# A third set of HGRN level operands, made one level earlier

## What is computed

```
def step(S, inp):
    qc, kc, vc, gc = inp
    b = jnp.cumsum(gc, axis=1)
    o_inter = jnp.einsum('bthk,bhkv->bthv', qc * jnp.exp(b), S)
    diff = b[:, :, None] - b[:, None, :]
    decay = jnp.where(tri, jnp.exp(jnp.where(tri, diff, 0.0)), 0.0)
    att = jnp.einsum('bthk,bshk,btshk->bhts', qc, kc, decay)
    o_intra = jnp.einsum('bhts,bshv->bthv', att, vc)
    b_last = b[:, -1]
    S = jnp.exp(b_last)[..., None] * S + jnp.einsum(
        'bshk,bshv->bhkv', kc * jnp.exp(b_last[:, None] - b), vc)
    return S, o_inter + o_intra
```

## Time and profile before

| | us |
|---|---|
| median of 3 runs | 1237.44 |
| lowest, highest | 1236.23, 1239.28 |
| profiled execution, its time | 1236.89 |
| its span, first to last instruction | 1235.1 |

### The profile page before, as it was taken

One profiled execution on the slowest core, in us unless ns is written; L12 is line 12 of the kernel. 1 busy time (PEld: TensorE's weight loads), 2 busy tenths in 40 slices (PEclk: granted clock), 3 DMA queues, 4 the chain that ended last, 5 costly groups with the idle time before them and its releaser, 6 DMA issues.

```text
span 1235.1 us, 22212 instructions
## 1 busy us (share of the span) xinstructions
PE 1146.0 (93%) x8917; PEld 1084.5 (88%) x8917; DVE 711.1 (58%) x1449; ACT 538.5 (44%) x950; POOL 182.3 (15%) x144
## 2 busy tenths in 40 slices
PE   5789999988999989999998999789999999999996
PEld 4688788966998978989988999589999999999996
DVE  5726554455487666476686655554463644636464
ACT  3433556456536555655535323453232232232334
POOL 1400000000133223213032001141011010110100
PEclk9889999999999988999998999799999999999997
DMA  9683322222322312222222155212323222222202
GB/s 313 199 315 103 103 69 93 80 73 77 136 84 71 105 42 64 71 67 73 71 69 71 62 192 185 69 35 69 103 69 103 69 76 96 70 102 70 92 12 77
DMA packets 108778, 120.46 MB, mean 98 GB/s; under 512 B 2692, under 2 KB 98652, under 8 KB 108389
## 3 DMA queue, kind: packets, MB, share of 16 engines
q1 hardware_dynamic: 108677, 119.06, 29.4%
HBM read 109.22 MB, written 11.80 MB: 98 GB/s over the span
## 4 chain that ended last, share of the span: by engine, by line
PE 47%; DVE 7%; ACT 2%; issue 1%; DMA 1%; POOL 0%; DVEq 0%; ACTq 0%; POOLq 0%
PE PS L763 41%; DVE wR L1288 1%; PE PS L877 1%; PE PS L722 1%; DMA xT<-residual 1%; DVE xhat L1256 1%; PE PS L923 1%; DVE qt L1441 0%; DVE tmp L1272 0%; PE PS L680 0%; DVE kt L1442 0%; DVE att L1459 0%; PE PS L930 0%; DVE tmp L1271 0%; PE PS L920 0%
## 5 line engine op out<-in xcount | busy, mean ns | idle before, releaser
L763 PE MATMUL PS<-hR,wR 128*128 128x288 f32 x3744 | 533.4, 300 | 12.8 <-ACT tmp L1069 6.7
L763 PEld LDWEIGHTS PS<-hR,wR 128*128 128x128 f32 x3744 | 509.5, 191 | 23.3 <-ACT tmp L1069 7.7
L763 PE MATMUL PS<-actR,wR 128*128 128x288 f32 x1920 | 258.8, 295 | 2.0 <-DVE actR L1425 1.8
L763 PEld LDWEIGHTS PS<-actR,wR 128*128 128x128 f32 x1920 | 255.4, 188 | 3.4 <-DVE actR L1425 2.0
L1288 DVE TENSOR_TENSOR wR<-raw,wR 128x512 fp32r<-128x512 f32 x256 | 205.0, 801 | 71.5 <-ACT wR L990 64.1
L990 ACT ACTIVATE wR<-raw 128x512 fp32r<-128x512 f32 x256 | 161.9, 632 | 140.6 <-PE PS L763 132.9
L1588 POOL TENSOR_TENSOR D<-b 128x512 f32<-128x512 f32 (+1 forms) x56 | 68.2, 1217 | 508.2 <-PE PS L850 267.9
L1615 POOL TENSOR_TENSOR actR<-tmp,actR 128x576 fp32r<-128x576 f32 x32 | 46.2, 1445 | 304.8 <-DVE actR L1341 304.8
L1341 DVE CAST actR<-tmp 128x576 fp32r<-128x576 f32 x32 | 15.2, 476 | 129.5 <-ACT tmp L1088 129.5
L722 PE MATMUL PS<-wR,hR 128*128 128x256 f32 x600 | 82.8, 296 | 2.0 <-ACT kT L1056 0.9
L722 PEld LDWEIGHTS PS<-wR,hR 128*128 128x128 f32 x600 | 77.5, 200 | 5.1 <-issue 1.7
(11 more groups left out here) (212 smaller groups left out, 1214.7 us busy)
## 6 DMA issues: line engine op xcount, KB each, us to landing
raw<-in_w_in SPq DMA_DIRECT2D x30, 1024.0 KB, 5.1
raw<-in_w_up SPq DMA_DIRECT2D x16, 1024.0 KB, 5.3
raw<-in_w_down SPq DMA_DIRECT2D x16, 1024.0 KB, 4.9
mid<-in_w_ada SPq DMA_DIRECT2D x12, 1024.0 KB, 5.1
ada<-in_w_ada SPq DMA_DIRECT2D x8, 1024.0 KB, 13.3
S<-in_state_hgrn SPq DMA_DIRECT2D x8, 512.0 KB, 4.5
out_hgrn_sample<-S SPq DMA_DIRECT2D x8, 512.0 KB, 5.2
raw<-in_w_out SPq DMA_DIRECT2D x4, 1024.0 KB, 4.9
```

The lines of the kernel that those rows point to most:

```text
L763: mm = pe.matmul(PS[:, 2 * x.pair + h, 0:HALF], weights(x, w, k, col), rhs[r], start=(k == 0 and n == 0), stop=(k == last and n == 2))
```

## The change

The operands get a third set (`qt2`, `kt2`), so the level uses set n % 3 in place of n % 2. In the slot of level n, `g_operands` is now for level n+2 (was n+1), `g_exp` for n+3 (was n+2) and `g_diff` for n+4 (was n+3). The second lead-in slot of a pair makes what is then missing: difference 3, operands 1 and exponential 2. The differences keep their three tiles, and the scores keep their two banks. `kt2` is cleared at its first use.

```
-    yield []
+    yield [("g_diff", first, 3), ("g_operands", first, 1), ("g_exp", first, 2)]
...
-                if n + 1 < 2 * NL:
-                    ev += [("g_operands", *at(n + 1))]
+                if n + 2 < 2 * NL:
+                    ev += [("g_operands", *at(n + 2))]
                 if k == 2:
                     ev += [("g_products", r)]
                 ev += [("g_level", r, k)]
-                if n + 2 < 2 * NL:
-                    ev += [("g_exp", *at(n + 2))]
                 if n + 3 < 2 * NL:
-                    ev += [("g_diff", *at(n + 3))]
+                    ev += [("g_exp", *at(n + 3))]
+                if n + 4 < 2 * NL:
+                    ev += [("g_diff", *at(n + 4))]
...
-                bank, q, k = A[l % 2], QTL[n % 2], KTL[n % 2]
+                bank, q, k = A[l % 2], QTL[n % 3], KTL[n % 3]
...
-                if n < 2:
+                if n < 3:
...
-                    done(dve.memset(KTL[n % 2][:], 0.0))
+                    done(dve.memset(KTL[n % 3][:], 0.0))
                 dve.wait_ge(s_E, n + 1)
-                if n >= 2:
-                    dve.wait_ge(s_lv, n - 1)
+                if n >= 3:
+                    dve.wait_ge(s_lv, n - 2)
```

More of the change, by code:

```diff
@@ L404, in program @@
             g_names += [(f"b{s}", [P, 2, TOK]), (f"kr{s}", [P, 2, TOK]), (f"qs{s}", [P, 2, TOK]), (f"rv{s}", [P, TT + 1, UC])]
-        (b0, kr0, qs0, rv0, b1, kr1, qs1, rv1, orec, D0, D1, D2, qt0, qt1, kt0, kt1, att, kh, eb, qh, khT, S, S0, S1, vblk) = stage(
-            *g_names, ("orec", [P, KT, TOK]), ("D0", [P, TOK]), ("D1", [P, TOK]), ("D2", [P, TOK]), ("qt0", [P, HALF]), ("qt1", [P, HALF]),
-            ("kt0", [P, TOK + SMP]), ("kt1", [P, TOK + SMP]), ("att", [P, TOK]), ("kh", [P, TOK]), ("eb", [P, TOK]),
+        (b0, kr0, qs0, rv0, b1, kr1, qs1, rv1, orec, D0, D1, D2, qt0, qt1, qt2, kt0, kt1, kt2, att, kh, eb, qh, khT, S, S0, S1, vblk) = stage(
+            *g_names, ("orec", [P, KT, TOK]), ("D0", [P, TOK]), ("D1", [P, TOK]), ("D2", [P, TOK]), ("qt0", [P, HALF]), ("qt1", [P, HALF]), ("qt2", [P, HALF]),
+            ("kt0", [P, TOK + SMP]), ("kt1", [P, TOK + SMP]), ("kt2", [P, TOK + SMP]), ("att", [P, TOK]), ("kh", [P, TOK]), ("eb", [P, TOK]),
             ("qh", [P, TOK]), ("khT", [P, TT + 1, P]), ("S", [P, TT, P]), ("S0", [P, NB, P]), ("S1", [P, NB, P]), ("vblk", [SMP, NB // 2, P]))
-        B, KR, QS, RV, D, QTL, KTL = [b0, b1], [kr0, kr1], [qs0, qs1], [rv0, rv1], [D0, D1, D2], [qt0, qt1], [kt0, kt1]
+        B, KR, QS, RV, D, QTL, KTL = [b0, b1], [kr0, kr1], [qs0, qs1], [rv0, rv1], [D0, D1, D2], [qt0, qt1, qt2], [kt0, kt1, kt2]
         osc = kh
@@ L1432, in g_operands @@
                 d = view(D[n % 3])
-                if n < 2:
+                if n < 3:
                     if n == 0:
                         dve.wait_ge(s_score, STEPS + 1)
-                    done(dve.memset(KTL[n % 2][:], 0.0))
+                    done(dve.memset(KTL[n % 3][:], 0.0))
                 dve.wait_ge(s_E, n + 1)
-                if n >= 2:
-                    dve.wait_ge(s_lv, n - 1)
-                done(dve.tensor_tensor(QTL[n % 2][:, 0:w // 2].rearrange("p (a m) -> p a m", m=m), view(q)[:, :, m:2 * m], d[:, :, m:2 * m], ALU.mult), s_Qt)
-                done(dve.tensor_tensor(view(KTL[n % 2])[:, :, 0:m], view(k)[:, :, 0:m], d[:, :, 0:m], ALU.mult), s_Kt)
+                if n >= 3:
+                    dve.wait_ge(s_lv, n - 2)
+                done(dve.tensor_tensor(QTL[n % 3][:, 0:w // 2].rearrange("p (a m) -> p a m", m=m), view(q)[:, :, m:2 * m], d[:, :, m:2 * m], ALU.mult), s_Qt)
+                done(dve.tensor_tensor(view(KTL[n % 3])[:, :, 0:m], view(k)[:, :, 0:m], d[:, :, 0:m], ALU.mult), s_Kt)
             def g_diag(r):
```

## The result

| | kernel before | changed kernel |
|---|---|---|
| median, 12 runs each, in turn on one chip | 1239.18 us | 1242.04 us |
| lowest, highest | 1235.55, 1242.89 | 1238.85, 1243.59 |
| profiled execution, its span | 1235.1 us | 1239.4 us |

The ratio is 1.0027, with a 95% interval of 1.0015 to 1.0039. The change costs some 3.3 us where the forecast was a gain of 4.6, and the result lies above the range.

A forecast was written before the change was run, and what follows sets the result against it. PE was taken to bound the kernel (busy 1146 of 1235 us). Head gains of 5.50 us less 0.9 for the lead-in, clock unchanged, gave -4.6 us: 1232.8 us on the median, range 1226.8 to 1238.7.

The forecast's parts named there:

- All eight waits of L877 go: Level matmuls on PE, 325 to 700 us: their eight waits for operands from DVE, 17.3 us in all, disappear.
- The waits move to keys, sample and output: PE would wait at keys (about 1.2, 3, 3, 2 us, heads 1, 3, 4, 7) and samples (about 5, 2, heads 2, 6).
- What each head gains: Per head, the smaller of PE's stalls and its tightest later step's margin on DVE; gains sum to 5.50 us.
- the four terms with `kh`: Heads 1, 3, 4 and 7, limited by when DVE ends `kh` for the keys: gains 1.08, 0.93, 0.11, 2.62 us.
- head 2: Sample matmuls limited by chunk states: margin 0.26 plus 0.5 from DVE work coming earlier, gain 0.76 of 5.68 us.
- What the lead-in adds: Two extra DVE multiplies before each pair's levels: 0.9 us in pair 3, delaying head 6's output; otherwise counted at 0.
- the rival "slower": Longer lead-in becomes the bound as multiplies run into POOL's work, 10.4 us lost in four pairs: about 1242, chance 0.07.
- The clock, "I take no net change": PE's half-rate stretches during or behind stalls: no net change, with -5 and +3.5 us as bounds.
- head 7's full gain: Keys of head 7: gain 2.62 us, from a 2.35 us stall and 1.7 us lost to slow clock behind it.
- Its bound, +3.5 us: Upper bound of the clock term: a slow stretch like the third, 1.7 us, occurring twice more.
- "leaves nothing": Rival: the wait moves with thinner gain, -1.9 us, as head 7's slow clock returns; about 1235.5, chance 0.37.
- the regained waiting, 2.9 us of the forecast: The part of the 4.6 us forecast gain that was waiting; the other 1.7 us was slow clock behind head 7's stall.

The follow-up runs named there:

- the lead-in alone: Kernel before, with only the change's second lead-in slot added (difference 3, operands 1, exponential 2 of each pair), two operand sets kept: ratio 0.9993.
- the later steps alone: Kernel before, with keys, states and samples one slot later and operands still one level ahead: ratio 0.9995.
- `kh` first: Changed kernel, with DVE making `kh` ahead of the operands of level n+2 in slot 2 of each head: ratio 1.003 to the kernel before.
- later steps: Changed kernel, with keys, states and samples one slot later (slots 4 to 7): median 1228.21 us, ratio 0.9911 to the kernel before.

## Why the prediction was wrong

- **All eight waits of L877 go:** right, 0.7 us are left on that line, none of it for L1441.
- **The waits move to keys, sample and output:** right, in every head named, and sized rightly: 1.34, 3.05, 2.64 and 2.34 us for the four pauses at the keys, 5.62 and 1.74 us at the samples. Three pauses were not named, 1.97 and 1.70 us at the keys of heads 2 and 6, each ahead of the sample's, and 1.02 us at the sample of head 0.
- **What each head gains:** right for the four terms with `kh` (1.04, 0.70, 0.11, 2.59 us against 1.08, 0.93, 0.11, 2.62). Wrong for head 2, -0.52 against +0.76: half of the first stall was to come back, and a diagonal copy that comes 1.75 us later in this pair outweighs it.
- **What the lead-in adds:** the mechanism was right, the size was not. The prediction charged two multiplies and only pair 3, 0.9 us. Measured were 1.7 us at the diagonal copy in both pair 1 and pair 3. It read DVE as idle in the lead-in of pair 1, where three weight parts stand, and it overlooked the difference that the operands release: POOL then works beside what DVE does next, a weight part in pair 1 and a merge in pair 3. A price for such a meeting stood in the rival "slower", 2.57 us for a pair of multiplies, but was laid on the multiplies alone; of these only one, in pair 3, met POOL (1.21 us). The Trainium skill (SBUF — State Buffer, "SBUF: two separate sides") has the two engines lock each other out of a shared port; the two L1288 of 2.25 us beside POOL's 1.59 us agree with it. As an experiment the lead-in alone still cost nothing (0.9993), so this term may shift time within the pair more than it decides the result.
- **The clock, "I take no net change":** this is the step that failed. In the profile 5.1 us are lost behind the steps, nearly all of it by slow stretches of 1.7 us there in heads 3, 4, 5 and 7, and in the means the clock loss rises by some 3.6 us (43.8 against 40.0 to 40.5) while the remainder stays. The other 2 us of the profile's miss in the HGRN slots are in the two terms above. The prediction saw that the pauses would be merged, and read it as neutral. But it had counted as gone the 1.7 us that followed head 7's stall, and they came back behind the new pause of 2.34 us, this time behind the keys. So "no net change" and head 7's full gain contradict each other: one of the two could hold. Nor did it ask what a merged pause does in heads 3 and 4. Its bound, +3.5 us, was about the rise that the means show; its central value was not. The Trainium skill (TensorE: Matmul & The Clock Gate, HAM oscillation) spoke against the change with the rule that a block behind a long enough pause starts at half rate. The rows behind 3.05, 2.34 and 5.62 us agree, those behind 1.34, 1.97 and 2.64 us (0.66 us for four matmuls of L887) show full rate directly after the pause, and behind the last the clock fell in the second profile all the same. The rule was taken as keeping the losses; measured, they grew, and filling the pauses took 8.3 us of clock loss from the changed kernel and 5.5 from the one before.
- **The rivals:** "leaves nothing" had the right mechanism, the slow clock behind head 7's keys and 0.5 us in each of pairs 1 and 2, and stopped 6 us short. "Slower" gave 1242, which was measured, from a cause that the experiments don't bear out: the 10.4 us of lead-in that it needed are some 1.7 us in two pairs. That its number was met is luck. The 0.07 for that side was too little, since an unpriced clock term of +3.5 us stood beside a gain of only 4.6.

**What stays open.** The stretch added in head 5 begins behind the output, without a pause ahead, in both profiles of the changed kernel; that of head 4 does so in one and follows a pause in the other. With filled pauses both are behind outputs, in the changed kernel and then in the kernel before too. So where the clock falls depends on more than the pause directly ahead, and no run here shows on what. That the pauses account for the difference is shown for the totals, within about 2 us, not stretch by stretch. That the regained waiting, 2.9 us of the forecast, didn't show in the remainder is measured; the steps of heads 2 and 6 account for 2.0 us of it in one profile, and the rest stays open.

## What to carry to other kernels

Where engines meet in a fixed order, list for one bound engine every step that waits for another and its margin, and give all of them room together: more room for the levels alone cost 0.3%, more for the later steps alone gave nothing, both gave 0.9%. Count a pause of TensorE by what follows it too, and where several short stalls turn into one long one, price the slow stretch behind it instead of calling it even; don't count slow clock as regained where a new pause stands right behind the old one. When a change moves waits about and the time barely reacts, split each run into time lost to the granted clock and the rest; then fill the pauses with matmuls nobody reads, in both kernels, to see which of the two moved.

## What the runs showed of the hardware

- More work took less time: 36 unread matmuls in the pauses cut 6 us from the changed kernel, and 32 cut 3.2 us from the kernel before.
- Pauses as short as 2.08 us (head 0, `kh` first) and 2.27 us (head 6, later steps) were followed by matmuls at half rate, 0.23 and 0.27 us each in place of 0.14. A pause of 2.64 to 2.66 us (head 4, changed kernel) was followed by full rate in one execution, 24 matmuls of L763 in 3.40 us, and by a fall of the clock in the next, the same 24 in 4.95 us. The length of the pause alone doesn't tell which.
- TensorE's clock also fell without a pause, behind the 8-column matmuls of an output: 24 matmuls of L763 in 4.96 us in place of 3.43, in head 5 of both profiles of the changed kernel, where the kernel before has them at the full clock in both of its own.
